# One token tile runs ahead from the second attention to the expert rows, the other three between its rows

## The chip, the cores and the metric

The kernel runs on one core of a Trainium2 chip. Its engines are TensorE (PE, with its weight loads shown apart as PEld), VectorE (DVE), ScalarE (ACT), GpSimd (POOL) and SyncE (SP), which work side by side and wait for each other on semaphores. The metric is the device time of one execution in microseconds (us), and less is better. Data is float32 throughout.

## What is computed

Two transformer blocks are applied to 512 tokens of width 1024. The change concerns the end of the second block: an attention over 768 keys, the merge with two other branches, an output projection, a layer norm, and a retrieval layer in which each token takes 8 x 16 = 128 of 16384 experts, each expert being a row `u` and a row `v` of 1024 numbers.

```python
def _peer(h, wq, k1, k2, u_tab, v_tab):
    def block(t):                                  # 128 tokens
        q = (t @ wq).reshape(PEER_BLOCK, PEER_HEADS, 2, PEER_DQ // 2)
        s1 = jnp.einsum('thd,nd->thn', q[:, :, 0], k1)
        s2 = jnp.einsum('thd,nd->thn', q[:, :, 1], k2)
        v1, i1 = lax.top_k(s1, PEER_TOPK)
        v2, i2 = lax.top_k(s2, PEER_TOPK)
        cand = (v1[..., :, None] + v2[..., None, :]).reshape(...)
        score, ci = lax.top_k(cand, PEER_TOPK)
        expert = i1[ci // 16] * PEER_NKEYS + i2[ci % 16]
        g = jax.nn.softmax(score, axis=-1)
        act = jax.nn.gelu(jnp.einsum('thkd,td->thk', u_tab[expert], t))
        return jnp.einsum('thk,thkd->td', g * act, v_tab[expert])

mix_x = _merge(gate, hgrn @ w_hg, conv @ w_cv, ox_att @ w_att_o, w_out)
x = _layer_norm_2(ALPHA * x + xg1 * mix_x, ln1_g, ln1_b)
x = _layer_norm_2(ALPHA * x + xg2 * _peer(_modulate(x, xsh2, xsc2), ...), ln2_g, ln2_b)
```

## The kernel before

Every engine has a program of its own, written out by hand as Python functions named after stage and engine (`attn2_tensor`, `wo_vector`, `peer_gpsimd`). What an engine does, it does in the order of these functions; semaphores alone tie the engines together. On-chip memory is one array (`arena`) cut by hand; weights stream through three panels of 2 MB, in the order of the list `ORDER`, each loaded by SP once the panel three places earlier is done with. A tile is 128 tokens, and there are four, `i` = 0 to 3.

The last stages follow one another, each for all four tiles:

- `attn2`: 32 units (4 tiles x 8 heads) in a software pipeline (`soft_tensor`, `soft_scalar`, `soft_vector`), tile 0 being units 0 to 7. A unit is a score product (L813), a maximum on DVE (L876), an exponential on ACT (L857), six transposes (L219) and six products with v (L831), and a scaled copy (L2056). Then the result is transposed for all tiles and `merge_tensor` runs 8 products with `w_at` (L251), each of 8 matmuls of 512 columns.
- `wo`: transposes (L219), 8 products with `w_o2` (L251), then on DVE the scaling by row (L2177), the residual (L2179), the layer norm (`norm_vector`, L2114 to L2121, with a square sum on ACT, L2125, and a power on POOL, L262) and the modulation (L2182, L2183), a tile at a time.
- `peer`: 16 products with `w_pq` (L257), each for all four tiles. Then the choice of the experts, a head of a tile at a time (`select_vector`, L2300 to L2351 on DVE, in 27 steps, fed by a score product L2256 on PE and a copy L2275 on ACT). Head h of tile i yields 16 row numbers a token.
- The rows: for each tile and each of its 128 places j, POOL issues one indirect DMA (L2438) that gathers 128 rows of 4 KB, a row for each token, into one of `NG` = 15 buffers (512 KB each). A gathered u row is multiplied with the token and summed on DVE (L2460, called a dot below). After `BL` = 8 dots the GELU is computed for them (L2465 to L2472, sigmoid on ACT L2413). A gathered v row is weighted and added in PSUM by two matmuls on PE (L2400), with a diagonal matrix made by ACT (L2418) as the other operand.

The order of the gathers is the list `FETCH`: 8 u rows, then u, v, u, v, the u rows 8 places ahead of the v rows. `in_order` walks all five programs along it: POOL issues gather n when step n - 14 is worked on, and between two rows the generator `chosen` is advanced by one step, which is one or two small DVE instructions of the choice. While the products with `w_pq` run, the choice is advanced too (8 steps for each), and POOL may issue the gathers whose row numbers are there and whose buffer is free; 12 of the 15 buffers are the panels of `w_pq`. After row 127 of a tile's v rows, the layer norm of that tile follows on DVE.

## Time and profile before

| what | us |
|---|---|
| median of 3 runs (4393.72 to 4408.49) | 4406.57 |
| the profiled execution, its own time | 4406.16 |
| its span in the trace | 4404.4 |
| attention 2 starts | 2559 |
| first gather of a row | 2851 |
| gathers without a break from | 2923 |
| last score product of the choice | 3994 |
| last gather issued | 4379 |

The span is the time from the first to the last instruction of the program; 1.8 us of the execution lie outside it. Start times in the rows are counted from the span's start. In a timeline a row gives start, duration, engine, line, operation and operands, and in square brackets how long the engine had been idle before and what ended that. PE counts twice as many matmul instructions in the trace as the program issues, because a float32 matmul is two of them.

### The profile page before, as it was taken

What the parts mean: (1) busy time and instruction counts of PE and PEld (TensorE: products, weight loads), DVE (VectorE), ACT (ScalarE), POOL (GpSimd) and SP (SyncE); (2) the same over time, 40 slices, a digit from 0 to 9 for tenths busy, and PEclk for the clock granted to TensorE, in tenths of its full rate; (3) what the DMA queues carried; (4) which work ended last, traced back from release to release, by engine and by line L of the source; (5) the groups of instructions that cost most, each with busy time, mean ns of one, the idle gap of its engine ahead of it and who ended that gap; (6) DMA issues with size and microseconds to landing.
All of it is one profiled execution on the core that took longest, in us unless ns stands there. A gap on an engine that the chain in (4) does not pass through costs nothing.

```text
span 4404.4 us, 33682 instructions
## 1 busy us (share of the span) xinstructions
PE 3692.0 (84%) x10702; PEld 1831.3 (42%) x10702; DVE 2225.5 (51%) x4995; ACT 867.8 (20%) x1836; POOL 1245.9 (28%) x1126
## 2 busy tenths in 40 slices
PE   8788899899999799984999999977776776776777
PEld 4345564444445356533654475432222222222222
DVE  0547532310001365986643543467767777766554
ACT  1223321200003222113211041112212221211111
POOL 0200000000000000000000000047777777777775
PEclk9875759999999998995999999999999998999999
DMA  3330001122221112220121203259999999999998
GB/s 154 137 144 1 31 28 39 67 77 76 76 76 57 53 58 75 89 100 0 58 86 58 96 20 135 72 168 366 369 363 350 369 367 338 353 351 368 383 408 335
DMA packets 167295, 743.18 MB, mean 169 GB/s; under 512 B 18728, under 2 KB 18728, under 8 KB 155984
## 3 DMA queue, kind: packets, MB, share of 16 engines
q0 software_dynamic: 154432, 574.82, 34.8%
q1 hardware_dynamic: 12672, 166.19, 10.3%
q8 instruction: 88, 1.44, 0.1%
q14 instruction: 87, 0.71, 0.0%
q10 hardware_dynamic: 16, 0.02, 0.0%
HBM read 724.16 MB, written 16.79 MB: 168 GB/s over the span
## 4 chain that ended last, share of the span: by engine, by line
PE 53%; DVE 16%; DMA 13%; issue 6%; POOL 4%; ACT 3%; DVEq 0%; POOLq 0%; ACTq 0%
PE ps L251 14%; DMA arena<-in_pu,arena 13%; PE ps L257 12%; PE ps L1335 6%; DVE arena L2460 6%; PE ps L1277 5%; POOL arena L2438 4%; PE ps L219 3%; PE ps L813 3%; PE ps L831 3%; PE ps L1559 2%; PE ps L1546 1%; PE ps L2400 1%; PE ps L443 1%; PE ps L910 1%
## 5 line engine op out<-in xcount | busy, mean ns | idle before, releaser
L2400 PE MATMUL ps<-arena 128*128 128x512 f32 x2048 | 1029.5, 638 | 426.8 <-ACT arena L2418 213.9
L2400 PEld LDWEIGHTS ps<-arena 128*128 128x128 f32 x2048 | 375.0, 198 | 1070.6 <-issue 548.5
L2460 DVE CUSTOM_DVE_ANT_0 arena<-arena 128x1024 f32<-128x1024 f32 x512 | 628.5, 1227 | 343.0 <-DMA arena<-in_pu,arena 317.4
L251 PE MATMUL ps<-arena 128*128 128x512 f32 (+1 forms) x1768 | 755.9, 589 | 11.0 <-DVE arena L244 7.9
L2438 POOL DMA_INDIRECT arena<-in_pv,arena x512 | 596.5, 1165 | 185.1 <-issue 119.8
L2438 POOL DMA_INDIRECT arena<-in_pu,arena x512 | 554.4, 1083 | 242.9 <-issue 61.2
L257 PE MATMUL ps<-arena 128*128 128x512 f32 (+1 forms) x1408 | 555.9, 557 | 3.1 <-DVE arena L1250 0.9
L251 PEld LDWEIGHTS ps<-arena 128*128 128x128 f32 x1768 | 337.4, 192 | 415.5 <-issue 409.3
L257 PEld LDWEIGHTS ps<-arena 128*128 128x128 f32 x1408 | 268.9, 191 | 287.4 <-issue 276.6
L262 POOL TENSOR_TENSOR arena<-arena 128x1 f32<-128x1 f32 (+7 forms) x38 | 61.1, 1609 | 1154.1 <-DVE arena L674 396.8
L219 PE MATMUL ps<-arena 128*128 128x128 f32 (+1 forms) x1094 | 208.8, 331 | 159.1 <-ACT arena L1636 59.9
L1335 PE MATMUL ps<-arena 128*128 128x512 f32 x640 | 293.6, 606 | 16.6 <-ACT arena L1636 12.8
L219 PEld LDWEIGHTS ps<-arena 128*128 128x128 f32 (+1 forms) x1094 | 154.0, 170 | 271.3 <-issue 114.9
L2418 ACT ACTIVATE arena<-arena 128x128 f32<-128x128 f32 x512 | 183.3, 394 | 317.7 <-PE ps L2400 287.9
L1277 PE MATMUL ps<-arena 128*128 128x512 f32 x512 | 220.2, 592 | 1.4 <-DVE arena L1304 1.4
L1359 POOL DMA_DIRECT2D aside<-arena x20 | 10.7, 534 | 720.9 <-ACT arena L1349 720.9
L1421 DVE SCALAR_TENSOR_TENSOR arena<-arena 128x512 f32<-128x512 f32 x240 | 180.6, 753 | 8.4
L813 PE MATMUL ps<-arena 128*128 128x256 f32 (+5 forms) x352 | 179.8, 618 | 1.5 <-ACT arena L1195 0.8
L1335 PEld LDWEIGHTS ps<-arena 128*128 128x128 f32 x640 | 118.8, 194 | 144.1 <-issue 125.8
L831 PE MATMUL ps<-arena 128*128 128x64 f32 (+1 forms) x928 | 163.1, 328 | 2.9 <-DVE arena L1042 2.0
L831 PEld LDWEIGHTS ps<-arena 128*128 128x128 f32 x928 | 156.0, 249 | 8.3 <-DVE arena L1042 2.7
L1277 PEld LDWEIGHTS ps<-arena 128*128 128x128 f32 x512 | 97.1, 190 | 123.7 <-issue 121.5
(300 smaller groups left out, 3021.6 us busy)
## 6 DMA issues: line engine op xcount, KB each, us to landing
arena<-in_w_in SPq DMA_DIRECT2D x27, 2048.0 KB, 8.4
arena<-in_w_ada SPq DMA_DIRECT2D x12, 2048.0 KB, 7.8
arena<-in_w_ff_in SPq DMA_DIRECT2D x8, 2048.0 KB, 7.9
arena<-in_w_ff_out SPq DMA_DIRECT2D x8, 2048.0 KB, 7.7
aside<-arena POOLq DMA_DIRECT2D x20, 512.0 KB, 5.7
arena<-in_w_pq SPq DMA_DIRECT2D x4, 2048.0 KB, 7.9
arena<-in_pu,arena POOLq DMA_INDIRECT x512, 6.2
arena<-in_pv,arena POOLq DMA_INDIRECT x512, 6.3
```

The costliest lines, as they stand in the source:

```text
L219: return t.transpose(ps, src, ID[0:src.shape[0], 0:src.shape[0]])
L251: x = t.matmul(PS[:, b, 0:n], hT[:, k, i * 128:(i + 1) * 128], w[:, k, :], start=k == 0, stop=k == nk - 1)
L257: x = t.matmul(PS[:, b, 0:n], w[:, k, f * 128:(f + 1) * 128], hT[:, k, 0:n], start=k == 0, stop=k == nk - 1)
L813: x = t.matmul(PS[:, b + c // 512, 0:w], u["q"], u["k"][:, c:c + w], start=True, stop=True)
L831: y = t.matmul(PS[:, b, 0:vv.shape[-1]], u_turned[st, jj][:, a * 128:a * 128 + 128], vv, start=a == 0, stop=a == len(u["v"]) - 1)
L1277: x = t.matmul(PS[:, 4 * c + i, :], AT[:, 8 * kk + k, 128 * i:128 * i + 128], w[:, k, :], start=kk == 0 and k == 0, stop=kk == 3 and k == 7)
L1335: x = t.matmul(PS[:, b, :], l, r, start=k == 0, stop=k == 7)
L1421: tap.V.own(v).scalar_tensor_tensor(out=cv, in0=u[:, j:j + 512], scalar=dw[:, 8 * j + k:8 * j + k + 1], in1=cv, op0=ALU.mult, op1=ALU.add) ...
L2400: x = t.matmul(PS[:, b + c, :], DG[j % 4], row(f)[:, 512 * c:512 * c + 512], start=j == 0, stop=j == 127)
L2418: a.activation(DG[j % 4], ID, ACT.Copy, scale=WG[i % 2][:, j:j + 1]).then_inc(*pe.A.step("dg", i, j))
L2438: g.indirect_dma_start(row(f), None, d[tab], bass.IndirectOffsetOnAxis(ap=EXU[i][:, j:j + 1], axis=0)).then_inc(s_gb[n % NG], 16)
L2460: pe.V.own(v).tensor_tensor_reduce(row(f), row(f), TT[:, i, :], 1.0, 0.0, ALU.mult, ALU.add, DOT[i % 2][:, j:j + 1]).then_inc(*pe.V.step(" ...
```

## The change

All of the change lies behind unit 10 of the second attention.

1. The tail of tile 0 (transposes, merge, `w_o2`, norm, `w_pq`, first head's choice, rows) becomes a generator, `rows_*`. `beside_attention` advances it by 2 steps after each attention unit from `HOOK` = 10 on: 16 steps of tile 0's tail and then 30 rows lie between attention units. PSUM banks 6 and 7 serve tile 0's tail.
2. Tiles 1 to 3 (`PARTS[1]`) go through the same tail together; one step of it runs after every third turn of the row loop, from row 30 on. A turn is one row, or, where a head isn't chosen yet, a turn without a row. Since the three panels are used twice, `w_at`, `w_o2` and `w_pq` are loaded twice (the names with a "+").
3. `FETCH` is new: 64 u rows alone, 64 u rows with a v row after every fourth, then four u rows to five v rows (by `goal`), and 16 v rows at the end. The GELU is taken for 16 rows at a time.
4. There are 7 row buffers for the first 144 rows and then 19. The choice advances by 2 steps a turn in the first 128 rows and by 1.5 after that.
5. The normalised x of each tile goes to memory (`XH`) and comes back before its second norm; rows of parameters are loaded in pieces, one set early (`rows_load`) and one late (`LATE`).

The core of the diff:

```diff
-                 + [("w_cv", 0), ("w_cv", 1), ("w_at", 0), ("w_at", 1), ("w_o2", 0), ("w_o2", 1)] + [("w_pq", c) for c in range(4)])
+                 + [("w_cv", 0), ("w_cv", 1)]
+                 + [(n + again, c) for again in ("", "+") for n, m in (("w_at", 2), ("w_o2", 2), ("w_pq", 4)) for c in range(m)])
...
+        PARTS = ((0,), (1, 2, 3))
+        PBANKS = ((6, 7), (0, 1, 2, 3))
...
+                if p == 0:
+                    b = bank(t, PBANKS[p], tl.A, "q", p, c)
+                    for f in range(4):
+                        for k in range(8):
+                            x = t.matmul(PS[:, b, 128 * f:128 * f + 128], w[:, k, 128 * f:128 * f + 128], h[:, k, :], start=k == 0, stop=k == 7)
...
+            def each(i):
+                g.wait_ge(*tl.V.at("var", i))
+                to_power(g, STo[:, 3:4]).then_inc(*tl.G.step("rstd", i))
+                if i == 2:
+                    g.wait_ge(s_xh[1], 16)
+                    load_x(3)
+                g.wait_ge(*tl.V.at("xn", i))
+                g.dma_start(XH[i], XR[i]).then_inc(s_xh[min(i, 2)], 16)
...
+        BL = 16
+        FETCH = []
+        done_v = 0
+        for n_ in range(1, 513):
+            FETCH.append(("pu", (n_ - 1) // 128, (n_ - 1) % 128))
+            goal = 0 if n_ < 64 else (n_ - 64) // 4 if n_ < 128 else 16 + (n_ - 128) * 5 // 4 if n_ < 512 else 512
+            while done_v < goal:
+                FETCH.append(("pv", done_v // 128, done_v % 128))
+                done_v += 1
...
+        FEW = len(PLACES)
+        PLACES += [panel("w_pq+", c)[:, 1024 * j:1024 * j + 1024] for c in (1, 2, 3) for j in range(4)]
+        MANY = len(PLACES)
+        FROM = 144
+        SPOT = [n % FEW if n < FROM else (n - FROM) % MANY for n in range(ROWS)]
...
-            for n in range(len(FETCH) + NG - 1):
-                if n < len(FETCH):
-                    while (FETCH[n][1], FETCH[n][2] // 16) not in ready:
-                        next(chosen)
-                    gather(FETCH[n])
-                if n >= NG - 1:
-                    yield FETCH[n - NG + 1]
-                    drain(chosen, 1)
...
+            def advance(r):
+                turns[0] += 1
+                drain(chosen, 2 if r < 128 or turns[0] % 2 else 1)
+                if r >= BESIDE and turns[0] % 3 == 0:
+                    drain(others, 1)
+            yield from first
+            n = 0
+            for r in range(ROWS):
+                while n < ROWS and PREV[n] < r:
+                    tab, i, j = FETCH[n]
+                    while tab == "pu" and (i, j // 16) not in ready:
+                        advance(r)
+                    gather(n)
+                    n += 1
+                yield FETCH[r]
+                advance(r)
+            drain(others, ALLSTEPS)
...
+        def beside_attention(work):
+
+            left = itertools.islice(work, FIRST + BESIDE)
+
+            def f(j):
+                if j >= HOOK:
+                    drain(left, 2)
+            return f
+        FIRST = 2 * len(pairs(0)) + 2 + 2 + 2 + 2 + 4
...
```

Where this moves instructions, first on POOL, from the end of the mixing stage to the first rows. Before, nothing but loads and the four powers of the norms (L262) stands ahead of the rows, and u and v rows take turns from the tenth on:

```order
52 L1827 DMA arena<-aside 128x2048 x2
53 L2103 DMA arena<-in_rows 128x8192
54 L2106 DMA arena<-ada_rows 128x4096
55 L2109 DMA arena<-x_spill 128x4096
56 L2110 DMA arena<-in_w_pk 128x256
57 L262 TENSOR_TENSOR arena<-arena 128x1 x4
58 L2438 DMA arena<-in_pu,arena 128x1024 x9
59 L2438 DMA arena<-in_pv,arena 128x1024
60 L2438 DMA arena<-in_pu,arena 128x1024
61 L2438 DMA arena<-in_pv,arena 128x1024
```

And after the change, the same place:

```order
58 L263 TENSOR_TENSOR arena<-arena 128x1
59 L2333 DMA x_norm<-arena 128x1024
60 L2589 DMA arena<-in_pu,arena 128x1024 x39
61 L2319 DMA arena<-aside 128x1536 x2
62 L2309 DMA arena<-x_spill 128x1024 x2
63 L2589 DMA arena<-in_pu,arena 128x1024 x29
64 L2589 DMA arena<-in_pv,arena 128x1024
65 L2589 DMA arena<-in_pu,arena 128x1024 x4
66 L2589 DMA arena<-in_pv,arena 128x1024
67 L2589 DMA arena<-in_pu,arena 128x1024 x4
```

One power and one store stand ahead of 39 gathers of u rows; the loads for the other tiles' tail come behind those, and the first v row is the 69th gather.

Then on PE, the end of the second attention. Before, its last unit is followed by the transposes, the merge, `w_o2`, transposes and `w_pq` of all tiles (L219, L251, L257):

```order
825 L219 MATMUL ps<-arena 128x128 x6
826 L831 MATMUL ps<-arena 128x128 x12
827 L219 MATMUL ps<-arena 128x128 x32
828 L251 MATMUL ps<-arena 128x512 x64
829 L219 MATMUL ps<-arena 128x128 x32
830 L251 MATMUL ps<-arena 128x512 x64
831 L219 MATMUL ps<-arena 128x128 x32
832 L257 MATMUL ps<-arena 128x512 x32
833 L2256 MATMUL ps<-arena 128x128 x4
834 L257 MATMUL ps<-arena 128x512 x56
```

After the change, between units 16 and 18 of the attention, with the first score product of the choice at its end (L2404, before L2256):

```order
768 L220 MATMUL ps<-arena 128x128 x6
769 L832 MATMUL ps<-arena 128x128 x6
770 L2167 MATMUL ps<-arena 128x128 x64
771 L814 MATMUL ps<-arena 128x512
772 L814 MATMUL ps<-arena 128x256
773 L220 MATMUL ps<-arena 128x128 x6
774 L832 MATMUL ps<-arena 128x128 x6
775 L2167 MATMUL ps<-arena 128x128 x64
776 L814 MATMUL ps<-arena 128x512
777 L814 MATMUL ps<-arena 128x256
778 L220 MATMUL ps<-arena 128x128 x6
779 L832 MATMUL ps<-arena 128x128 x6
780 L2404 MATMUL ps<-arena 128x128 x4
```

Tile 0's product with `w_pq` is 128 matmuls of 128 columns (L2167) in two pieces between attention units, and the first head's choice starts with 14 units of the attention still to come.

## Rows read from the trace of the kernel before

**Rows 1.** The page: busy tenths in 40 slices of 110 us, with GB/s.

```profile
PE   8788899899999799984999999977776776776777
DVE  0547532310001365986643543467767777766554
POOL 0200000000000000000000000047777777777775
GB/s 154 137 144 1 31 28 39 67 77 76 76 76 57 53 58 75 89 100 0 58 86 58 96 20 135 72 168 366 369 363 350 369 367 338 353 351 368 383 408 335
```

**Rows 2.** Stretches of the end: length, busy us (instructions) by engine, clock, DMA share, GB/s.

```profile
2559.00:2670.00 111.00, 107.15 (x729) 88.71 (x729) 53.27 (x130) 59.56 (x134) 2.40 (x5) 1.00 0.03 10
2670.00:2734.00 64.00, 58.85 (x160) 27.65 (x160) 18.39 (x25) 7.40 (x7) 0.87 (x2) 1.00 0.53 217
2734.00:2806.00 72.00, 62.77 (x160) 29.56 (x160) 39.79 (x45) 8.11 (x15) 2.20 (x4) 0.90 0.16 59
2806.00:2923.00 117.00, 114.92 (x273) 51.34 (x272) 36.38 (x144) 13.31 (x26) 11.22 (x12) 0.97 0.20 68
2923.00:4100.00 1177.00, 819.07 (x1697) 310.93 (x1698) 855.77 (x2221) 240.44 (x587) 927.99 (x799) 0.93 0.96 355
4100.00:4378.00 278.00, 209.71 (x432) 74.11 (x431) 142.57 (x284) 40.98 (x122) 212.16 (x217) 1.00 1.02 407
```

**Rows 3.** The same view for the gathers (L2438) alone.

```profile
2923.00:4100.00 1177.00, 926.25 (x796) 0.93 0.96 355
4100.00:4300.00 200.00, 152.45 (x157) 1.00 1.02 407
2923.00:4378.00 1455.00, 1138.41 (x1012) 0.95 0.97 365
```

**Rows 4.** Timeline of POOL: the last norm and the first gathers.

```profile
2798.35 0.54 POOL L262 TENSOR_TENSOR arena<-arena 128x1 f32<-128x1 f32 x1 [13.19 <-DVE arena L2118]
2850.64 1.05 POOL L2438 DMA_INDIRECT arena<-in_pu,arena  x1 [51.75 <-DVE arena L2347]
...
2899.37 0.93 POOL L2438 DMA_INDIRECT arena<-in_pu,arena  x1 [0.30 <-issue]
2922.66 0.93 POOL L2438 DMA_INDIRECT arena<-in_pv,arena  x1 [22.36 <-DVE arena L2304]
```

**Rows 5.** Timeline, DVE without a pause: gathers beside dots and steps of the choice.

```profile
3318.74 1.40 POOL L2438 DMA_INDIRECT arena<-in_pu,arena  x1 [0.30 <-PE ps L2400]
3320.44 1.81 POOL L2438 DMA_INDIRECT arena<-in_pv,arena  x1 [0.30 <-issue]
3322.55 1.79 POOL L2438 DMA_INDIRECT arena<-in_pu,arena  x1 [0.30 <-issue]
...
3318.10 1.23 DVE L2460 CUSTOM_DVE_ANT_0 arena<-arena 128x1024 f32<-128x1024 f32 x1
...
3320.20 1.23 DVE L2460 CUSTOM_DVE_ANT_0 arena<-arena 128x1024 f32<-128x1024 f32 x1
3321.36 0.08 DVE L2460 DVE_READ_ACCUMULATOR2_ANT arena<- 128x1 f32 x1
...
3322.30 1.23 DVE L2460 CUSTOM_DVE_ANT_0 arena<-arena 128x1024 f32<-128x1024 f32 x1
```

**Rows 6.** Timeline, the choice over, dots waiting for their rows.

```profile
4202.37 1.00 POOL L2438 DMA_INDIRECT arena<-in_pu,arena  x1 [0.30 <-PE ps L2400]
4203.67 0.95 POOL L2438 DMA_INDIRECT arena<-in_pv,arena  x1 [0.30 <-issue]
4203.89 1.23 DVE L2460 CUSTOM_DVE_ANT_0 arena<-arena 128x1024 f32<-128x1024 f32 x1 [1.34 <-DMA arena<-in_pu,arena]
```

**Rows 7.** Timeline of PE, ACT and DVE: an attention unit, merge, norm of a tile, `w_pq`, first head.

```profile
2655.87 0.96 DVE L876 TENSOR_REDUCE arena<-ps 128x1 f32<-128x768 f32 x1 [0.94 <-PE ps L813]
2659.16 0.96 DVE L876 TENSOR_REDUCE arena<-ps 128x1 f32<-128x768 f32 x1 [0.94 <-PE ps L813]
...
2665.56 3.69 PE L219 MATMUL ps<-arena 128*128 128x128 f32 x32 [0.54 <-DVE arena L2056]
2669.94 55.20 PE L251 MATMUL ps<-arena 128*128 128x512 f32 x128 [0.69 <-ACT arena L235]
...
2751.52 0.69 DVE L2177 TENSOR_TENSOR arena<-ps,arena 128x512 f32<-128x512 f32 x1 [6.12 <-PE ps L251]
2759.08 1.23 DVE L2121 TENSOR_TENSOR arena<-arena 128x1024 f32<-128x1024 f32 x1
...
2839.85 0.30 DVE L2300 MAX8 arena<-arena 128x8 f32<-128x128 f32 x1 [35.86 <-ACT arena L2275]
2850.39 0.23 DVE L2347 TENSOR_SCALAR arena<-arena 128x16 f32<-128x16 f32 x1
```

**Rows 8.** End of the kernel: last gather, last sum, store.

```profile
4378.62 0.95 POOL L2438 DMA_INDIRECT arena<-in_pv,arena  x1 [0.30 <-issue]
4392.03 1.22 DVE L2476 TENSOR_TENSOR arena<-ps,arena 128x1024 f32<-128x1024 f32 x1 [15.97 <-PE ps L2400]
4401.36 0.33 SPq L2569 DMA_DIRECT2D out_y<-arena  x1
```

679 lines of the change are left out of this document (406 added, 273 removed).

## The prediction

> **What bounds the kernel now.** I read the page's slices first: from slice 27 on POOL is at 0.7 to 0.8, DVE at 0.5 to 0.7, PE at 0.6 to 0.7, and 335 to 408 GB/s arrive; before slice 26 POOL does almost nothing [rows 1]. So the last third of the time is a stage of its own, the gathers. The table by stretch splits the end: 364 us from the second attention to 2923 in which PE is busy for 344 us in sum, then 1455 us of gathers [rows 2]. To see what bounds the gathers I took them alone: 796 in 1177 us, busy 926 us, which is 1.164 us each; the 0.30 us that stands ahead of every one (rows 5 and 6 show it whatever it is put down to) makes 1.464, and the measured step is 1177 / 796 = 1.479 us [rows 3]. POOL thus has no time left: it issues without a break, and its own issue is the bound, not a buffer and not the dots. The timeline tells why an issue takes 1.16 us and not the 0.94 of the first ones [rows 4]: an issue that starts while a dot runs ends 0.81 us after that dot ends. The one at 3320.44 began 0.24 us into the dot of 3320.20 (1.23 long, so over at 3321.43) and ended at 3322.25; the next did the same with the dot of 3322.30 [rows 5]. An issue that starts just ahead of a dot isn't held: at 4203.67 it took 0.95, the dot began at 4203.89 [rows 6]. When the choice is over, dots wait for their rows, fall into this place by themselves, and the step is 278 / (1012 - 796) = 1.287 us at 407 GB/s [rows 2, 3, 6].
>
> The Trainium skill (SBUF — State Buffer, "SBUF: two separate sides") has the rule behind this: DVE instructions that hold the port pair shared with GpSimd keep GpSimd from writing descriptors. The trace agrees in kind, with 0.81 us from the dot's end to the issue's end. The same page (its part on the bandwidth-pool intuition) gives some 358 GB/s as a core's share of HBM; by that a 512 KB row could not take less than 1.464 us, and gathers would gain nothing from a quieter DVE.
>
> **The change, stage by stage.** Sums are made on the trace's own clock.
>
> *A, until tile 0 can choose experts.* Attention starts at 2559 and a unit takes 3.29 us, set by PE (107 of 111 us busy; two scans lie 3.29 apart) [rows 2, 7]. Ten units and the start-up put the first piece of tile 0's tail at 2595. Up to unit 17, PE does 8 more units (26 us), 24 transposes of two instructions at 3.69 / 32 = 0.115 us (5.5), two products for `w_at` and two for `w_o2` at 55.20 / 8 = 6.9 us (27.6), and tile 0's `w_pq`: 128 matmuls, 256 instructions of 128 columns. Nearest to these are the transposes, 0.115 us, against 0.43 (55.20 / 128) for 512 columns; I take 0.125, 32 us, and 110 as the other end. Waits: the norm chain of a tile, from 2751.52 to 2760.31, is 8.8 us [rows 7], and PE has one unit and two idle steps to put beside it, so 7 us stay; six sums of rows on DVE, 7.4 us, cost about 5. The panels load 7 to 8 us each while 8 us of `w_pq` run, so nothing for them. 2595 + 26 + 5.5 + 27.6 + 32 + 12 = 2698, say 2700.
>
> *B, tile 0's u rows.* Here every row is a dot, DVE has no pause, and it is the bound. With two steps of the choice a turn a row takes 2.1 us: the dots start 2.10 apart [rows 5]. Its work until row 144 (128 dots, 16 v rows): 128 dots at 1.23 + 0.08 + 0.1 of gaps = 181 us; nine heads, from 2839.85 to 2850.62 plus two small steps, 11.6 us each with the starts between dots, 105 [rows 7]; 16 attention units still to come at 53.27 / 32 = 1.66 us busy, 29 with gaps; eight GELUs, 10; the tail of three tiles, (18.39 + 39.79 - 7) / 4 = 13 us a tile, 38, with waits for square and power 43 [rows 2]; waits for PE 8. Sum 376 us, so row 144 at 3076. PE has about 53 us of attention and 185 of the other tiles' tail in that time (twelve products at 6.9, sixteen of 384 columns at 5.2, transposes), so it stays beneath DVE. POOL needs one issue for a dot and gets one, held or not. Seven buffers are enough: six rows of 2.1 us against some 6 us of landing. POOL's waits for the norms (`each`) are covered by the same six rows. The second loading of eight panels (16.8 MB) and the trips of x (4 MB) fall here, where 144 rows (75 MB in 376 us) leave the DMA engines half empty: nothing. Ends for B: 330, if the gaps vanish and the attention's DVE work finds room; 440, if each of the tails' hand-overs stalls a turn.
>
> Then 10 us at the switch to 19 buffers: POOL waits for the last of the `w_pq+` products, loses its lead, and one landing (6 us) shows.
>
> *C, the choice beside mixed rows.* 23 heads at 28 steps, 1.5 a turn, are 429 turns; I take 420 rows. A dot now comes with 2.25 rows, not 2. Undisturbed the issue costs 0.95 + 0.30 = 1.25 us [rows 6]; before, the dots add (1.479 - 1.25) x 2 = 0.46 us each. With 0.444 dots a row: 1.25 + 0.444 x 0.46 = 1.455 us, 611 us in all. DVE would need 0.444 x 1.41 + 1.5 x 0.415 = 1.25 us a row and stays beneath. Ends: 1.25 (no dot holds an issue; 525 us) and 1.716 (each dot costs the longest hold, 1.99 - 0.94 = 1.05, the longest issue of the trace; 721 us).
>
> *D, rows alone.* 1024 - 144 - 420 = 460 rows. Before, only the last 216 gathers are of this kind, since the choice of the last tile ends near 4000. At 1.287 us less the small difference in dots, 1.283: 590 us. If dots didn't fall into place it would be C's 1.455, 669 us.
>
> *Rest.* 11 more direct DMAs on POOL in C and D, at 0.85 with their gap: 8 us. From the last gather to the end of the span 25 us [rows 8]; the last v rows no longer wait for a GELU, but 16 of them lie behind each other at 1.7 us against 1.3 for issuing, which takes that back.
>
> Sum: 2700 + 376 + 10 + 611 + 590 + 8 + 25 = 4320 in the span, against 4404. Outside the span lie 1.8 us, and the profiled execution was 0.4 below the median, so 4322; I write 4320. As a check by gains: at 3076 the kernel before has issued 11 + 153 / 1.479 = 114 gathers, the new one 144, worth 44 us; D has 244 more rows at 0.17 less, 42; C's rows give 10; the switch and the extra DMAs take 18.
>
> **Rivals.**
> 1. *The hold grows.* With 1.5 steps of the choice a row DVE is near 88% in C, against 856 of 1177 us, 73%, before [rows 2]. If dots queue up, they start at once one after the other and not on a landing; every dot may then catch an issue at its start, as three in a row do at 3318 to 3322 [rows 5], and the new rhythm of four to five may keep D from falling into place. C at 1.716 and D at 1.455: 4320 + 110 + 79 = 4509. It decides from 0.65 us a dot: the 86 us of gain are used up when 880 rows cost 1.46 on average. For it: DVE's load. Against it: a queue of dots means that POOL is ahead, and POOL is never ahead here. Chance 0.13.
> 2. *B is longer*: DVE, PE and ACT hand over in strict order in the attention, with two rows between units; B at 440 and A 10 more give 4394. Chance 0.12.
> 3. *The gathers speed up further*: 19 buffers, half the GELUs, B at 335 and C at 1.36 a row (4320 - 41 - 40): 4239. Chance 0.12.
> 4. *The transfer is the bound*: the DMA share is 0.96 while the choice runs, and 355 GB/s would be what memory gives, with or without holds. C and D would then take 880 x 1.479 = 1302 us instead of 1201: 4421. Against it: 407 GB/s over 278 us [rows 2]. Chance 0.03. (The HBM share on the page named above is this rival's rule; it would give 880 x 1.464 = 1288 us and 4407.)
>
> **Numbers.** The forecast, 4250 to 4385, has 0.60. Above about 4393 or below it by 0.3% of 4406 a measurement can just tell a difference. Faster: 0.60, 0.12 for the third, two thirds of the second: 0.80. Same: the rest of the second and the slow edge of the first: 0.07. Slower: the first and most of the fourth rival, less what of the first stops short of 4420: 0.13. The range runs from 4230 to 4400; it leaves out the first rival and little of the others.
>
> **What would show it.** First u gather near 2710; row 144 (the last dot of tile 0) near 3076 with DVE over 0.9 busy until then; after that POOL's gathers without a break, mean length 1.15 us, until about 3700, then 0.98 at 407 GB/s; DVE pausing for landings from 3700 on. A first gather after 2750, or a dot of tile 1 after 3140, makes A or B wrong; mean lengths over 1.3 us make C wrong, and a D at over 1.1 us makes the fourth term wrong.

## The result and the profile after

The changed kernel takes 4365.93 us (median of 5 runs, 4363.67 to 4373.84) against 4408.34 of the kernel before on the same chip: a ratio of 0.9913, interval 0.9893 to 0.9934. It is faster, by 0.7 to 1.1%, and by half of what was forecast: 42 us where 86 were forecast. Its profiled execution took 4371.77 us, its span is 4370.0.

The page of the changed kernel, busy tenths in 40 slices of 109 us with GB/s, answers to [rows 1]:

```profile
PE   8788899899999799993999997476877678788787
DVE  0547532310001356895652544885478778544443
POOL 0200000000000000000000101335377777777775
GB/s 152 140 146 1 14 45 39 52 76 75 77 96 58 53 58 53 104 79 29 45 80 76 80 119 192 218 243 273 176 406 368 352 365 385 368 408 409 368 406 320
```

Rows arrive from slice 25 on (counted from 0, as in the prediction), at 218 to 273 GB/s while tile 0's u rows run; before, 366 GB/s set in with slice 27. Then comes a slice with 176, at the change from 7 to 19 buffers. Behind it 352 to 409 GB/s arrive, but for the last slice; three of the last six slices have 406 to 409, before it was one.

The stretches, in the columns of [rows 2] (length, busy us and instructions of PE, PEld, DVE, ACT and POOL, clock, DMA share, GB/s). The bounds are the first gather, tile 0's last dot, gather 200, the end of the choice (last MAX8) and the last gather:

```profile
2706.00:3094.00 388.00, 251.59 (x806) 141.75 (x807) 289.85 (x717) 68.42 (x139) 165.37 (x157) 0.82 0.69 236
3094.00:3203.00 109.00, 87.12 (x213) 39.52 (x211) 57.92 (x167) 19.95 (x47) 58.85 (x62) 0.95 0.71 265
3203.00:3716.00 513.00, 400.23 (x885) 162.85 (x886) 416.03 (x1178) 111.41 (x284) 399.90 (x362) 0.94 0.99 374
3716.00:4340.00 624.00, 496.89 (x1039) 185.24 (x1038) 280.87 (x504) 104.27 (x280) 475.73 (x470) 0.98 1.01 394
```

The same view for the gathers (L2589) alone, the answer to [rows 3]; in the third row no tile ends, in the second one does:

```profile
3203.00:3716.00 513.00, 398.14 (x359) 0.94 0.99 374
3760.00:3812.00 52.00, 38.39 (x33) 0.97 0.92 337
3812.00:4060.00 248.00, 188.98 (x192) 1.00 1.03 408
```

Beside the choice a gather steps at 513 / 359 = 1.43 us, behind it at 1.34 on average, and at 248 / 192 = 1.29 where no tile ends. Starts of single instructions, in us, gathers counted from 0, the forecast counted as its sum does:

| | before | forecast | after |
|---|---|---|---|
| first gather | 2851 | 2700 | 2706 |
| tile 0's last dot | 3275 | 3076 | 3094 |
| gather 144 | 3121 | 3086 | 3076 |
| gather 160 | 3144 | 3109 | 3147 |
| gather 200 | 3201 | 3167 | 3203 |
| choice over | 4051 | 3697 | 3716 |
| gather 800 | 4091 | 4000 | 4039 |
| last gather | 4379 | 4295 | 4339 |
| end of the span | 4404 | 4320 | 4370 |

The rows start 145 us sooner, and at gather 200 the changed kernel is 2 us late. (Traces of kernels that are alike up to the first gather have it anywhere from 2695 to 2709, so a difference of a few us between starts in two traces says nothing.) From gather 200 to the last there are 823 steps; they took 1178 us before and 1137 after. So the whole gain of the profiled execution lies there, and nothing of the head start is left. 823 steps at the undisturbed 1.277 us (what most groups of 16 gathers behind the choice have, 1.274 to 1.285) would be 1051 us: 127 us of disturbance before, 86 after.

**Where the head start goes.** Timeline of POOL at the change of buffers (the 45 us by which it leads the kernel before at gather 144 are gone at gather 160):

```profile
3093.51 0.95 POOL L2589 DMA_INDIRECT arena<-in_pv,arena  x1 [16.52 <-DVE arena L2619]
...
3102.63 0.95 POOL L2589 DMA_INDIRECT arena<-in_pv,arena  x1 [6.38 <-DVE arena L2456]
...
3145.32 0.94 POOL L2589 DMA_INDIRECT arena<-in_pu,arena  x1 [26.35 <-PE ps L258]
```

Three stops, 49 us. The last waits for L258, the products of the other tiles with `w_pq+`, whose panel is the buffer. The other two wait for buffers that dots hold. The first of them, 16.52 us, lies behind a stop of DVE itself of 15.74 us; during the second DVE works off the dots and steps that this stop had held up. DVE's rows, ACT's and two of PE's for the same time:

```profile
3091.27 0.16 DVE L2498 RECIPROCAL arena<-arena 128x1 f32<-128x1 f32 x1 [15.74 <-ACT arena L2429]
...
3139.42 0.16 DVE L2498 RECIPROCAL arena<-arena 128x1 f32<-128x1 f32 x1 [14.88 <-ACT arena L2429]
3136.99 0.49 ACT L2214 ACTIVATE arena<-ps 128x384 f32<-128x384 f32 x1 [8.74 <-PE ps L258]
3139.08 0.21 ACT L2429 ACTIVATE arena<-arena 128x16 f32<-128x16 f32 x1
3073.41 26.03 PE L258 MATMUL ps<-arena 128*128 128x384 f32 x80
...
3131.61 5.34 PE L258 MATMUL ps<-arena 128*128 128x384 f32 x16
```

DVE wants the exponential of the choice (L2429). ACT has it behind its copies of the `w_pq+` products (L2214), which wait for PE, and PE does the sixteen products, with a few v rows between them, from 3029 to 3145. DVE's second stop, 14.88 us, costs nothing more: POOL waits for the panel until 3145 anyway.

**Where the rows behind the choice lose.** DVE and POOL at the end of tile 1:

```profile
3753.95 0.15 DVE L2648 TENSOR_SCALAR arena<-arena 128x1 f32<-128x1 f32 x1 [1.31 <-ACT arena L2561]
3762.61 0.87 DVE L2650 TENSOR_SCALAR arena<-arena 128x1024 f32<-128x1024 f32 x1 [8.50 <-POOL arena L263]
...
3768.21 1.22 DVE L2619 CUSTOM_DVE_ANT_0 arena<-arena 128x1024 f32<-128x1024 f32 x1
...
3769.35 1.22 DVE L2619 CUSTOM_DVE_ANT_0 arena<-arena 128x1024 f32<-128x1024 f32 x1
3761.99 0.59 POOL L263 TENSOR_TENSOR arena<-arena 128x1 f32<-128x1 f32 x1
3762.75 0.98 POOL L2589 DMA_INDIRECT arena<-in_pu,arena  x1 [0.18 <-issue]
3767.41 1.69 POOL L2589 DMA_INDIRECT arena<-in_pv,arena  x1 [3.68 <-DVE arena L2619]
3769.40 1.98 POOL L2589 DMA_INDIRECT arena<-in_pu,arena  x1 [0.30 <-issue]
```

The variance is there at 3754.1. POOL's power on it stands in its queue behind gathers that run ahead, so DVE waits 8.50 us. Meanwhile dots pile up; they then run 1.15 us apart, and each issue is held to 1.98 us, with a stop for a buffer of 3.68 us. 16 gathers from 592 on step at 1.88 us, the next 16 at 1.38. The same at gather 816, with 1.73, 1.42, 1.38 and 1.38 us in four groups of 16. Over 1.277 us a row the two places cost some 24 us together. Between the last dot ahead of the norm and the first behind it DVE is away for 22 us. No run takes its wait for the power away, so how much of the loss is the wait and how much is DVE's own work for the norm stays open.

**The end.** PE's last v rows, the last gather, the first sum on DVE, as in [rows 8]:

```profile
4333.54 23.35 PE L2542 MATMUL ps<-arena 128*128 128x512 f32 x54
4339.27 0.94 POOL L2589 DMA_INDIRECT arena<-in_pv,arena  x1 [0.30 <-issue]
4356.93 1.22 DVE L2642 TENSOR_TENSOR arena<-ps,arena 128x1024 f32<-128x1024 f32 x1 [31.41 <-PE ps L2542]
```

From the last gather to the end 30.7 us, forecast 25.

### The profile page after: what moved, and what is told of

Read it like the earlier page. It is cut to its first block, busy times and chain, and to the rows that moved or that the text cites. A ratio compares the mean times of both kernels' runs of the same rounds, so it can differ in the third digit from the quotient of the medians.

```text
span 4370.0 us, 33503 instructions
## 1 busy us (share of the span) xinstructions
PE 3684.3 (84%) x10958; PEld 1877.5 (43%) x10958; DVE 2180.5 (50%) x4839; ACT 846.3 (19%) x1788; POOL 1195.4 (27%) x1151
## 4 chain that ended last, share of the span: by engine, by line
PE 49%; DVE 20%; POOL 9%; DMA 8%; issue 6%; ACT 3%; POOLq 0%; DVEq 0%; ACTq 0%
PE ps L252 13%; PE ps L258 9%; POOL arena L2589 8%; DMA arena<-in_pu,arena 5%; PE ps L1278 5%; PE ps L1336 5%; DVE arena L2619 5%; DVE arena L1422 4%; PE ps L2542 3%; PE ps L220 3%; PE ps L814 2%; PE ps L1560 2%; PE ps L832 2%; DMA arena<-in_pv,arena 2%; PE ps L1547 1%
## 5 line engine op out<-in xcount | busy, mean ns | idle before, releaser
L2542 PE MATMUL ps<-arena 128*128 128x512 f32 x2048 | 1001.8, 631 | 320.5 <-DMA arena<-in_pv,arena 159.3
L2619 DVE CUSTOM_DVE_ANT_0 arena<-arena 128x1024 f32<-128x1024 f32 x512 | 623.5, 1221 | 377.8 <-DMA arena<-in_pu,arena 376.7
L252 PE MATMUL ps<-arena 128*128 128x512 f32 (+1 forms) x1768 | 759.8, 590 | 31.4 <-ACT arena L2108 24.4
L2542 PEld LDWEIGHTS ps<-arena 128*128 128x128 f32 x2048 | 379.0, 197 | 925.4 <-issue 518.1
L2589 POOL DMA_INDIRECT arena<-in_pu,arena x512 | 540.6, 1056 | 372.3 <-issue 82.8
L2589 POOL DMA_INDIRECT arena<-in_pv,arena x512 | 545.4, 1065 | 193.3 <-issue 107.3
L258 PE MATMUL ps<-arena 128*128 128x512 f32 (+2 forms) x1408 | 527.1, 536 | 3.1 <-DVE arena L1251 0.9
L252 PEld LDWEIGHTS ps<-arena 128*128 128x128 f32 x1768 | 339.0, 193 | 437.4 <-issue 432.2
L220 PE MATMUL ps<-arena 128*128 128x128 f32 (+1 forms) x1094 | 218.1, 339 | 212.6 <-ACT arena L858 70.5
L258 PEld LDWEIGHTS ps<-arena 128*128 128x128 f32 x1408 | 267.8, 190 | 261.8 <-issue 219.4
L1336 PE MATMUL ps<-arena 128*128 128x512 f32 x640 | 293.5, 606 | 16.6 <-ACT arena L1637 12.8
L1278 PE MATMUL ps<-arena 128*128 128x512 f32 x512 | 220.2, 592 | 1.4 <-DVE arena L1305 1.4
L1336 PEld LDWEIGHTS ps<-arena 128*128 128x128 f32 x640 | 118.7, 194 | 144.1 <-issue 125.8
L832 PE MATMUL ps<-arena 128*128 128x64 f32 (+1 forms) x928 | 172.4, 342 | 8.0 <-DVE arena L2115 5.1
L832 PEld LDWEIGHTS ps<-arena 128*128 128x128 f32 x928 | 165.3, 263 | 13.6 <-DVE arena L2115 5.3
L1278 PEld LDWEIGHTS ps<-arena 128*128 128x128 f32 x512 | 97.1, 190 | 123.7 <-issue 121.5
```

The costliest lines, as they stand in the source:

```text
L220: return t.transpose(ps, src, ID[0:src.shape[0], 0:src.shape[0]])
L252: x = t.matmul(PS[:, b, 0:n], hT[:, k, i * 128:(i + 1) * 128], w[:, k, :], start=k == 0, stop=k == nk - 1)
L258: x = t.matmul(PS[:, b, 0:n], w[:, k, f * 128:(f + 1) * 128], hT[:, k, 0:n], start=k == 0, stop=k == nk - 1)
L832: y = t.matmul(PS[:, b, 0:vv.shape[-1]], u_turned[st, jj][:, a * 128:a * 128 + 128], vv, start=a == 0, stop=a == len(u["v"]) - 1)
L1278: x = t.matmul(PS[:, 4 * c + i, :], AT[:, 8 * kk + k, 128 * i:128 * i + 128], w[:, k, :], start=kk == 0 and k == 0, stop=kk == 3 and k == 7)
L1336: x = t.matmul(PS[:, b, :], l, r, start=k == 0, stop=k == 7)
```

## The experiments

The kernels ran in five groups, each on a chip of its own beside the kernel before. Its median was 4405.5, 4401.6, 4395.8 and 4404.5 us on four of the chips, and 4461.6 on the fifth. So kernels of different groups are compared by their ratio to it. Intervals in brackets are 95% intervals.

### What eats the head start: the other tiles' tail

My theory was that the `w_pq+` products come too late and too dense; its rival, that seven buffers are too few. First, a tail step after every second turn:

```diff
-                if r >= BESIDE and turns[0] % 3 == 0:
+                if r >= BESIDE and turns[0] % 2 == 0:
```

> The changed kernel with one number altered: the tail of tiles 1 to 3 advances a step after every second turn of the row loop, not after every third. Theory 1 (late w_pq+): at the switch to tile 1 the sixteen w_pq+ products (5.3 us each on PE, 85 us) stand packed between 3040 and 3147; DVE waits for an exponential that stands on ACT behind the copies of these products, POOL waits 26 us for the panels that become its row buffers. With the tail done 43 turns earlier the switch loses 30 to 45 us less, and tile 0's stage gets 0 to 20 us longer: 4335 to 4355 against 4366. Theory 2 (few buffers): the loss at the switch is POOL's lead, lost with 7 buffers and refilled at the speed of issue, and PE has nothing to do with it: the switch stays, tile 0's stage gets longer, 4370 to 4390.

Measured 4353.78 us, ratio 0.9883 (0.9817 to 0.9950). The waits of POOL between 3094 and 3203 (sum, times, longest), first of the changed kernel, then of this one:

```profile
POOL arena L2589 <- PE ps L258: 26.7, 2, 26.3
POOL arena L2589 <- DVE arena L2619: 16.5, 1, 16.5
```

```profile
POOL arena L2589 <- DVE arena L2619: 9.1, 2, 5.6
```

The last product ends at 3070 instead of 3145, tile 0's last dot comes 9 us later, and gather 200 is issued at 3185 instead of 3203. Counted from the first gather it is 482 us against 497. The time lies in the range of theory 1, but its interval holds the 0.9913 of the changed kernel, so the gain rests on the traces; those of later runs with this tail pace have 481 to 487 us up to gather 200 (the chip with 4461.6 left out), those with every third turn 500 and 501.

Then half of the `w_pq+` product (4 of 8 matmuls in each, so those tiles choose by half a product):

```diff
-                        mm_feat(t, b, h, 8, w, f, 384).then_inc(*tl.P.step("q", p, 4 * c + f))
+                        mm_feat(t, b, h, 4, w, f, 384).then_inc(*tl.P.step("q", p, 4 * c + f))
```

> The changed kernel with the sixteen w_pq+ products of tiles 1 to 3 cut to 4 of their 8 matmuls each (half of that product is left out, so the choice of experts of these tiles is another; the rows gathered are as many). PE's packed stretch shrinks from 85 to 43 us. Theory 1: the pauses of DVE (15.7 and 14.9 us before L2498) and of POOL (26 us) shrink by about half, 4325 to 4345. Theory 2: nothing but a PE that idles more, 4361 to 4371.

Measured 4335.53 us, ratio 0.9840 (0.9779 to 0.9900). 42 us less work for PE brings the last dot of tile 0 from 3094 to 3070 and gather 200 from 3203 to 3165. Counted from the first gather, the last dot comes 19 us sooner, and from the last dot to gather 200 it takes 95 us instead of 109. POOL's wait for L258 falls from 26.7 to 12.8 us. From there to the last gather nothing changes: 1137 us in both. So the loss up to gather 200 goes by that product, as theory 1 has it.

A finer setting of the pace, every third turn until row 80, every second from there:

```diff
-                if r >= BESIDE and turns[0] % 3 == 0:
+                if r >= BESIDE and turns[0] % (2 if r >= 80 else 3) == 0:
```

> The changed kernel with a step of the other tiles' tail after every third turn of the row loop as before until row 80, and after every second turn from row 80 on. In the run with every second turn from row 30 on, the last w_pq+ product came 74 us sooner and the time fell to 4353.8, but tile 0's last dot came 10 us later (3103 against 3093.5). Theory (late w_pq+: the switch to 19 buffers is late because of the last eight panels' products, not because of the tail as a whole): the first half of the tail costs the dots nothing at the old pace, so the last dot stays at 3090 to 3097, the last w_pq+ product ends near 3100, row 200 is gathered at 3180 to 3190, and the time is 4345 to 4355, as good as or a little better than every second turn throughout. Rival (what counted there was the earlier start of the other tiles' choice, so the choice is over sooner): gathers up to row 200 as in the changed kernel, and a time of 4360 to 4368.

A miss: 4364.86 us, ratio 0.9930 (0.9899 to 0.9962), no better than the changed kernel. The last dot comes at 3103, and the last product at 3118 is still behind gather 144 (3101), with a stop of 18 us on POOL; gather 200 is at 3201. Counted from the first gather, the last dot comes after 395 us, between the 388 of every third turn and the 400 of every second. Gather 200 and the time are what the rival had forecast. Its cause doesn't fit the run with every second turn, though: there 15 us are won before gather 200 and 4 behind it, so the earlier end of the choice brought little. That the late last product is why this pace doesn't pay is my reading of three paces, not shown by a run of its own.

The changed kernel without the overlap, `HOOK` = 34, so that tile 0's tail follows the whole attention:

```diff
-        HOOK = 10
+        HOOK = 34
```

> The changed kernel with tile 0's tail and first rows put behind the whole second attention (HOOK = 34), all else as it is. Theory 1: attention ends at 2668 as before the change, tile 0's tail of about 85 us follows, so the first gather moves from 2706 to about 2760; DVE has no attention work beside the rows any more (29 us less), so tile 0's stage is shorter: 4366 + 54 - 29 = 4391, 4383 to 4400. Rival (the overlap costs what it brings, since PE, ACT and DVE hand over in strict order): 4360 to 4372.

Measured 4406.28 us, ratio 1.0022 (0.9987 to 1.0057), 6 us above the range of theory 1 and far from the rival's. The first gather is at 2760, as expected, 54 us later, but gather 200 only 34 (3237): the row stretch until the last dot takes 365 us instead of 388, 22 us less where 29 were expected. From gather 200 to the last it takes 1134 us, as in the changed kernel. So without the overlap the change gains 43 us behind gather 200, but is 36 us late by then; the overlap is what makes it pay.

v rows from the 32nd u row on, with the few buffers kept until row 160:

```diff
-            goal = 0 if n_ < 64 else (n_ - 64) // 4 if n_ < 128 else 16 + (n_ - 128) * 5 // 4 if n_ < 512 else 512
+            goal = 0 if n_ < 32 else min((n_ - 32) * 5 // 4, n_ - 16) if n_ < 512 else 512
-        FROM = 144
+        FROM = 160
-                if f == ("pv", 0, 24):
+                if f == ("pv", 0, 64):
```

> The changed kernel with v rows from the 32nd u row on, five to four until they are 16 places behind the u rows, then in turn with them; 19 buffers from row 160 on, not 144. Theory 1: in tile 0's stage POOL idles between dots (step 2.5 us against 1.25 of work), v rows there cost it nothing; at tile 0's last dot some 80 rows more are issued, of which PE and the 7 buffers take back a part: 4300 to 4345. Rival (7 buffers): v rows hold buffers while PE is in a product of 6.9 us, dots wait for landings, tile 0's stage gets longer by as much: 4366 to 4400.

My expectation missed: 4404.74 us, ratio 0.9985 (0.9951 to 1.0018), a little above the rival's range too. At tile 0's last dot, 3281, 244 gathers are out against 146, but gather 200 is at 3218, 15 us later than in the changed kernel, and behind it 823 steps take 1154 us. Reading ahead only u rows, which the change does, is no loss.

Last, on the version with the tail at every second turn and the spread norm (below), 19 buffers from gather 128 on:

```diff
-        FROM = 144
+        FROM = 128
```

> The version with the spread norm and the tail at every second turn (4321.96), with 19 buffers from gather 128 on instead of 144. There the last w_pq+ product ended at 3063, when POOL had issued 131 gathers, and POOL took 2.3 us a gather up to the 144th for want of buffers; behind the switch POOL issues without a break and is the bound. Theory (the few buffers cost POOL its lead from the moment at which the panels are free): gathers 128 to 160 step at 1.3 to 1.5 us, the 200th is issued 15 to 20 us sooner than at 3179, and all that follows with it: 4300 to 4310. Rival (DVE, not POOL, sets the rows until about the 200th, so a lead won there is waited off again at the 19th buffer, or the panels come free too late): 4317 to 4327.

> The version with the spread norm and the tail at every second turn, with 19 buffers from gather 128 on. Theory (want of buffers costs POOL its lead once the panels are free): the 200th gather 15 to 20 us sooner than in that version on this chip, and the total with it. Rival (DVE sets the rows there, or the panels come free too late, so the lead is waited off again): within 5 us of it. In the last run of it, on the slow chip, gathers 128 to 160 took until 3131 against 3132 in the version with 144, which speaks for the rival; I expect it now.

The first run fell on the chip with 4461.6 and stands at 4422.98, ratio 0.9932 (0.9899 to 0.9965), which says little without its partner there. The second: 4336.48 against 4333.16 us for 144 on the same chip, ratio 0.9855 against 0.9811; from the first gather to the last 1602 and 1600 us. My later expectation holds: there is no want of buffers at that point, once the product is early.

### What a row costs: the hold

The step of 1.48 us beside the choice was put down to dots that hold POOL's issues (an issue that starts while a dot runs ends some 0.8 us after the dot). Dots over half the columns (half of each u.x product left out; the rows are fetched whole), in the kernel before (L2460) and in the changed one (L2619):

```diff
-                    v.tensor_tensor_reduce(row(f), row(f), TT[i], 1.0, 0.0, ...
+                    v.tensor_tensor_reduce(row(f)[:, 0:512], row(f)[:, 0:512], TT[i][:, 0:512], 1.0, 0.0, ...
```

> The kernel before, with every dot taken over 512 of the 1024 columns of the row and of the token (half of each u.x product is left out; every row is still fetched whole). Nothing else moves. The question is whether the dots' hold on POOL's issues sets the 1.479 us step while the choice runs. Hold theory: a dot then lasts about 0.65 us instead of 1.23, fewer issues start inside one and those that do are let go earlier, so the mean issue falls from 1.16 us towards 1.0 and the step from 1.479 to 1.33 (1.28 to 1.38): over the 796 rows before 4100 that is 119 us, total near 4287 (4240 to 4330). Once the choice is over, the step stays at 1.28 to 1.29. Rival (the transfer is the bound while the choice runs, 355 GB/s being what memory gives beside other work): the step stays at 1.479 and the time at 4395 to 4410.

> The changed kernel with dots over 512 of the 1024 columns again (half of each u.x product left out), on another chip than the one with 369 GB/s. Hold theory, where over 400 GB/s arrive: the time from gather 200 to the last falls from 1137 us to about 1075 (1071 in the kernel before with half dots; 823 steps of 1.277 would be 1051), the last dot of tile 0 comes 25 to 45 us sooner than 3093, and the total is 4255 to 4290, ratio 0.970 to 0.978. Rival (the dots' length is not what the rows cost): from gather 200 to the last 1110 us or more and a total over 4310.

The kernel before: 4264.81 us, ratio 0.9707 (0.9626 to 0.9789). The changed one: 4282.05 us, ratio 0.9734 (0.9661 to 0.9808). Both lie in the range of the hold theory. Gathers alone, beside the choice: the kernel before as it is, the kernel before with half dots, the changed one with half dots (length, busy, clock, DMA share, GB/s):

```profile
3201.00:4051.00 850.00, 669.31 (x576) 0.94 0.97 357
```

```profile
3162.00:3916.00 754.00, 570.17 (x580) 0.98 1.02 405
```

```profile
3173.00:3649.00 476.00, 359.52 (x365) 0.98 1.03 408
```

Steps of 1.476, 1.300 and 1.304 us at 357, 405 and 408 GB/s: shorter dots alone let the rows come faster, so the dots' hold and not the transfer set the step. The mean issue falls from 669.31 / 576 = 1.16 us to 570.17 / 580 = 0.98, which is the whole difference of the steps. With half dots the kernel before steps at 1.30 us behind the choice too, so the choice's own small instructions cost the gathers next to nothing. The DMA share is 0.97 to 1.03 in all three and tells nothing here. The time from gather 200 to the last is 1071 us in the kernel before and 1068 in the changed one, against 1178 and 1137 with whole dots. So without the hold the change gains 3 us there instead of 41, and as a whole nothing (0.9734 against 0.9707, with overlapping intervals). Its gain is hold taken away: 359 rows beside the choice behind gather 200 instead of 576. With whole dots POOL is busy with these gathers for 918 us before and 871 after.

The first run of the changed kernel with half dots fell on the chip with 4461.6:

> The changed kernel with every dot taken over 512 of the 1024 columns (half of each u.x product is left out, every row is fetched whole). It asks two things. First, what bounds the stretch of tile 0's u rows, forecast at 376 us with DVE over 0.9 busy and measured at 394 with DVE at 0.78. If DVE is the bound there, the last dot of tile 0 comes 128 x 0.6 = 77 us sooner, near 3017. If the engines' hand-overs and PE's part of the other tiles' tail are, it comes at 3060 to 3090. I now expect the second, near 3060. Second, the rows behind the choice's start: by the hold theory the step between gathers 200 and 600 falls from 1.44 us to 1.30 (as it fell from 1.479 to 1.302 in the kernel before), 56 us, and that behind the choice from 1.341 to 1.31, 14 us: total 4255 to 4290. Rival (the transfer bounds those rows): 1.42 to 1.44 and a total of 4330 to 4365.

4409.81 us, ratio 0.9866 (0.9788 to 0.9943): both expectations missed, since each was for the other chips. Gathers beside and behind the choice there:

```profile
3179.00:3712.00 533.00, 369.37 (x367) 0.87 0.97 367
3712.00:4371.00 659.00, 442.08 (x457) 0.88 0.97 366
```

A gather is as short as with half dots elsewhere (442.08 / 457 = 0.97 us), but the step is 1.44 to 1.45: POOL is ahead and stops for buffers. On that chip, in these runs, the transfer is the bound, the fourth rival's case. Tile 0's last dot came at 3070, as expected; the pace-1 kernel below, which is the changed kernel up to there, has it at 3101 on the same chip.

### How fast the choice should go

The prediction's forecast has rows beside the choice at a price of their own; the question was whether a faster choice is always better. All three settings are compared on the version with spread norm and tail at every second turn (next section); with 1.5 steps a turn it is that version itself.

```diff
-                drain(chosen, 2 if r < 128 or turns[0] % 2 else 1)
+                drain(chosen, 2)
```

> The version with the spread norm and the tail at every second turn (4321.96), with the choice at 2 steps a turn from row 128 on instead of 1.5; the choice then ends some 107 rows sooner, near 3510. If the cost goes by the rows beside the choice, 107 rows fall from 1.43 to 1.28 us, 16 us: 4300 to 4312. If it goes by the steps: 4317 to 4327. If a fuller DVE (near 0.9) makes the dots queue up and catch an issue each, as the first rival of the prediction has it: 4330 and more, with a mean gather of over 1.3 us until 3510.

> The same version with the choice at 2 steps a turn. Cost by rows beside the choice: 107 rows fewer, 16 us less than the version before it on this chip. Cost by the choice's steps: within 5 us of it. DVE too full (dots queue and each catches an issue): 8 us or more slower than it, with a mean gather of over 1.2 us until the choice is over. On a chip where the transfer is the bound: the same or slower.

> The version with the spread norm and the tail at every second turn (0.9811 and 0.9851 of the kernel before, 1111 and 1115 us from gather 200 to the last), with the choice at 1 step a turn from row 128 on. At 1.5 steps 326 rows beside the choice step at 1.395 us, at 2 steps 236 rows at 1.512. If what a row costs goes by how full DVE is, 1 step a turn gives some 500 rows at 1.32 to 1.34 and 1100 to 1115 us from gather 200 to the last, ratio 0.979 to 0.986. If it goes by the number of rows beside the choice, some 500 rows at 1.40 and more (1.478 in the kernel before at this pace): 1130 to 1150 us, ratio 0.987 to 0.993. I find the two about equally likely.

Pace 1 (`2 if r < 128 else 1`) on the changed kernel came first, on the chip with 4461.6:

> The changed kernel with the choice at 1 step a turn from row 128 on instead of 1.5, so that it ends some 220 rows later (near 4000). It tells whether what a row costs goes by the rows that lie beside the choice or by the choice's steps themselves. If by the rows (dots find no place between issues as long as any choice work runs): 220 rows go from 1.28 to about 1.42 us, 20 to 30 us more: 4380 to 4400. If by the steps (each small DVE step displaces a dot by so much, whatever the pace): the sum is the same and the time stays at 4360 to 4372.

There it took 4470.66 us, ratio 1.0013 (0.9981 to 1.0044), and pace 2 on the other version 4442.92, ratio 0.9978 (0.9939 to 1.0018). The first misses both of its theories; the second has the time of the third theory (4330 and more), but a mean issue of 1.12 us and not over 1.3. Neither tells the pace, since the transfer is the bound there. The others: pace 2 4356.96 us, ratio 0.9878 (0.9810 to 0.9946), against 4333.16, ratio 0.9811, for 1.5 on the same chip; pace 1 4339.78 us, ratio 0.9873 (0.9799 to 0.9947). All engines from gather 200 to the end of the choice at 1, 1.5 and 2 steps a turn:

```profile
3177.00:3911.00 734.00, 570.93 (x1240) 219.61 (x1239) 514.66 (x1327) 157.53 (x384) 575.48 (x526) 0.97 0.99 379
```

```profile
3193.00:3646.00 453.00, 358.17 (x800) 145.14 (x800) 375.34 (x1064) 99.71 (x257) 354.03 (x328) 0.95 1.00 382
```

```profile
3184.00:3540.00 356.00, 264.13 (x581) 116.27 (x582) 309.57 (x929) 70.78 (x192) 266.77 (x238) 0.89 0.95 355
```

DVE is busy for 0.70, 0.83 and 0.87 of the time, for 521, 325 and 236 gathers: 1.41, 1.39 and 1.51 us each. From gather 200 to the last: 1130, 1115 and 1134 us. From 1 to 1.5 the cost goes by the number of rows beside the choice: the price of a row stays, and there are 196 rows fewer. At 2 DVE is too full, as the third theory had it, and the version is 24 us slower than with 1.5; but the mean issue stays under the 1.2 us that this theory asked for. The price rises, more by stops (1.51 less a mean of 266.77 / 238 = 1.12 on POOL leaves 0.39, not 0.30) than by longer issues (1.08 at 1.5). Intervals of the ratios overlap, so the order of 1 and 1.5 rests on the traces alone.

### The end of a tile, and the best version

The second norm of tiles 0 to 2 in three parts behind the next tile's v rows 6, 10 and 14 (sums and mean; variance; scaling and output), with ACT's square and POOL's power; the core on DVE, where a part once stood behind row 127:

```diff
+        END = (6, 10, 14)
...
-                if f and tab == "pv" and j == 127:
+                if f and tab == "pv":
+                    now = (0, 1, 2) if (i, j) == (3, 127) else (END.index(j),) if i and j in END else ()
+                    e = i if j == 127 else i - 1
+                    for part in now:
```

> The changed kernel with the second norm of tiles 0, 1 and 2 not behind the tile's last v row, but in three parts behind the next tile's v rows 6, 10 and 14: the sums and the mean, the variance, the scaling and output. ACT's square and POOL's power go with it. In the changed kernel the gathers step at 1.38 to 1.88 us for about 64 rows from each such place on, against 1.28 elsewhere once the choice is over: 11 to 13 us for each of two tile ends in that stretch (gathers 592 to 624 and 816 to 880). Theory (the dots are stopped for some 10 us there by DVE's waits for square and power, and with them the buffers): steps of 1.28 to 1.30 all through, and some 8 us less for each of three ends: 4342 to 4352. Rival (the slow steps there come of DVE's extra work or of the dots losing their place between issues, which spreading does not take away): 4362 to 4370, with the slow steps moved some rows on.

4358.15 us, ratio 0.9910 (0.9863 to 0.9957): a miss by 6 us at least, and by its ratio no faster than the changed kernel. The trace shows the direction: behind the choice a row steps at 1.312 instead of 1.341, 14 us on 465 rows. DVE at the new place:

```profile
3770.56 0.15 DVE L2656 TENSOR_SCALAR arena<-arena 128x1 f32<-128x1 f32 x1
...
3788.48 0.86 DVE L2659 TENSOR_SCALAR arena<-arena 128x1024 f32<-128x1024 f32 x1 [10.16 <-POOL arena L263]
```

The wait for POOL's power is still there, 10.16 us: the power stands behind up to 18 gathers, and four v rows are too little distance. What is left of the slow steps at tile 1's end is one group of 16 gathers at 1.61 us (from 608) where there were two at 1.88 and 1.38; at tile 2's end it is 1.33 and 1.43 where there were four of 1.38 to 1.73. Between two dots DVE is now away for at most 14 us, not 22, and behind gather 160 POOL no longer stops at all, where it stopped for 11 us in all. So a shorter break in the dots costs less, as the theory has it, though the slow steps also moved some rows on, as the rival has it.

Both together, tail at every second turn and spread norm:

> The changed kernel with both: a step of the other tiles' tail after every second turn of the row loop, and the second norm of tiles 0 to 2 in three parts behind the next tile's v rows 6, 10 and 14. The two losses lie in different stretches (rows 128 to 200, and the tile ends behind gather 590), so their gains should add: 12 us of the first, as measured alone, and what the norm's spreading brings by itself, expected 24: 4325 to 4340, faster than both kernels. Rival (the gains overlap, since an earlier choice only makes POOL wait elsewhere): 4345 to 4355.

> The version with the spread norm and the tail at every second turn again (it was at 0.9851 of the kernel before). Where rows behind the choice come at 1.28 us: 0.982 to 0.987 of the kernel before, some 40 us under the changed kernel. Where the transfer bounds them: 15 to 25 us under the changed kernel, from the earlier switch alone, since the stops at a tile's end are then made good by the transfers that are queued.

> The changed kernel itself, beside the kernel before, to be compared with the three that follow on the same chip. The last four runs were on a chip on which the gathers stood at 1.44 to 1.48 us a row even with half dots (mean issue 0.98 us, 369 GB/s), so that the transfer was the bound there. By the hold theory a chip with over 400 GB/s in the last third gives 4360 to 4370 and a ratio of 0.990 to 0.994 to the kernel before. If this is again a chip with some 369 GB/s, the rows behind the choice cost what those beside it cost, the 42 us that the prediction had from them go, and the ratio is 0.995 to 1.003.

4321.96 us, ratio 0.9851 (0.9764 to 0.9938), and in the second run 4333.16, ratio 0.9811 (0.9749 to 0.9873). The changed kernel again, on the chip of the second run: 4365.29 us, ratio 0.9945 (0.9905 to 0.9986). So on the same chip the combination is 32 us under the changed kernel and faster than both. The first run is 3 us under the expected range, the second is 32 us under the changed kernel where 40 were expected, and the changed kernel's ratio is at the edge of its range. From its first gather to gather 200 the combination takes 486 us instead of 500, the rest 1115 instead of 1138.

## Why the prediction was half right

The forecast gain is 86 us and the measured one 42. The largest terms that failed are the switch of buffers (10 us forecast, 28 measured) and the price of a row in D (1.283 us forecast, 1.341 measured).

**The direction and the bound** were right: from gather 160 on POOL issues with 11 us of stops in all, and its issue is what counts. The rival "the transfer is the bound" fell on the two chips where half dots brought 405 and 408 GB/s beside the choice; it holds on the one with 366 GB/s. On the others only the rows behind the choice speak against it, with 405 to 409 GB/s. By an estimate from the Trainium skill's share of HBM (SBUF — State Buffer, the bandwidth-pool part, 358 GB/s a core) no gather would take less than 1.464 us; the runs show 1.29 at 408 GB/s, and even the slow chip 1.44 at 366.

**A was right**: first gather at 2706, forecast 2700 in the sum, and 2695 to 2709 in the traces with the same code.

**B was mis-sized by 12 us and its bound was wrong.** From the first gather to tile 0's last dot it takes 388 us (390 in the second trace of the changed kernel), forecast 376; with A's 6 us the last dot is 18 us late. The step said that DVE has no pause and is the bound. DVE is busy for 290 of the 388 us, 0.75, not over 0.9. Where it waits there (sum, times, longest):

```profile
DVE arena L2263 <- PE ps L252: 23.9, 5, 6.7
DVE arena L2498 <- ACT arena L2429: 21.5, 7, 15.7
DVE arena L2619 <- DMA arena<-in_pu,arena: 19.6, 16, 3.3
```

Three causes of like size: the other tiles' residual waits for PE's product, the choice for ACT, the dots for rows. Taking 77 us of dots away shortened the stretch from the first dot to the last by 28 us (355 against 383); taking 42 us from PE, by 20. So the work of one engine counts there for less than half; hand-overs in a fixed order explain that, but no run alters the order. The 8 us set down as "waits for PE" were the term at fault: DVE stands idle for 98 us in all. The sum had 368 us for its work with gaps, where it is busy for 290, and that hid most of the error.

**The switch, 10 us, is a step that failed.** The prediction had POOL wait for the last `w_pq+` product and lose one landing. It priced the products of the other tiles (sixteen at 5.2 us) as work that PE has time for, without asking when they come. They came in a block of 116 us, from 3029 to 3145, with gather 144 (3076) in it and its end 51 us behind tile 0's last dot. From the forecast's 3086 for gather 144, POOL was 10 us ahead of it at 3076 and 38 behind at gather 160. Against the forecast for gather 200 (3167), 36 us were lost: 18 up to the last dot, 18 here, so the switch cost 28 us and not 10.

**C, 1.455 us a row, was right**: 1.43 measured (mean issue 1.11, forecast 1.15), 9 us better over 359 rows, and the choice ended at gather 559 of the forecast's 564.

**D, 1.283 us a row, is the other step that failed, 27 us too low** for 465 rows at 1.341. The undisturbed value holds (1.28 to 1.29). Missing were the two tile ends. The prediction read D's price from the 278 us behind 4100, in which no tile ends. But the kernel before has a tile end just ahead of 4100, behind its choice: DVE waits for POOL's power there too, an issue is held for 2.01 us, and 16 gathers from 784 on step at 1.73 us.

```profile
4071.17 1.29 DVE L2120 SCALAR_TENSOR_TENSOR arena<-arena 128x1024 f32<-128x1024 f32 x1 [5.63 <-POOL arena L262]
4071.31 2.01 POOL L2438 DMA_INDIRECT arena<-in_pu,arena  x1 [0.18 <-issue]
4076.17 0.95 POOL L2438 DMA_INDIRECT arena<-in_pv,arena  x1 [2.85 <-DVE arena L2332]
```

All 248 gathers behind the choice of before take 327 us, 1.319 each; with this price D would have been 607 us and not 590, which is 17 of the 27 us. The prediction's check by gains comes to 78 us, not 84 (4404 less 4320). It counted 44 us at the start, all of which were lost, and 42 + 10 of the rows, where 41 came.

**The end** was 6 us too short: the 16 last v rows on PE take 1.73 us each (23.35 us for 13.5 rows), and nothing of POOL's time covers the last ones.

Sum of the misses: 6 + 12 + 18 - 9 + 27 + 6, less the 8 us for extra DMAs, which the forecast counted apart and the measured steps contain, is 52; with five rows more in D than in C and the rounding it is the 50 from 4320 to 4370.

The first rival (dots that queue up catch an issue each) was real but local: at each tile end for some 30 gathers, and with the choice at 2 steps a turn in milder form. Its turning point doesn't follow from its own figures: 880 rows at 1.46 us are 0.21 over 1.25, and with 384 dots among them that is 0.49 us a dot, not 0.65.

## What to carry to other kernels

A stage that is bound by one queue gains from a head start only if the resource for its later pace is free when the head start arrives: price a background job by when its last instruction comes, not by whether the engine has room for its sum. A price per row that is read from a stretch must be read from one that holds every kind of event of the stage, here a tile's end. A small operation on the engine that issues the transfers stands behind all that it issues ahead: give its reader more distance than the lead of the queue. (The first of these rests on runs; for the last, four v rows were shown to be too few, and no run tried more.)
